# Three layer-norm joints of a two-block transformer kernel: GpSimd makes the shift, two engines empty PSUM in turn, modulation rows and kept rows are placed elsewhere

## The reference

```python
def first_block(x, ...):
    for l in range(2):
        mix = token_mixing(x, w_in[l], ...)              # attention branches, then @ w_o
        x = layer_norm(ALPHA * x + mix, ln1_g[l], ln1_b[l])
        ffn = conv_ffn(x, w_up[l], conv_w[l], conv_b[l], w_down[l])
        x = layer_norm(ALPHA * x + ffn, ln2_g[l], ln2_b[l])
    return x

def second_block(x, c, ctx, c_ctx, ada_w, ada_b, ...):
    for i in range(2):
        m_lat = silu(c) @ ada_w[i] + ada_b[i]            # modulations, width 6 * 1024
        m_ctx = silu(c_ctx) @ ada_w[i] + ada_b[i]
        h = _rms(x, norm1_g[i]) * (1.0 + sc1) + sh1      # slices of m_lat, m_ctx
        ...
```

## Time and profile before

| | |
|---|---|
| median of 3 runs | 3923.62 us (3922.15 to 3926.23) |
| the profiled execution's own time | 3922.99 us |
| its span, from first to last instruction | 3920.8 us |
| PE busy, share of the span | 3644.1 us, 93% |
| DVE busy | 2035.2 us, 52% |
| ACT busy | 1444.3 us, 37% |
| POOL busy | 185.0 us, 5% |

### The profile page before, as it was taken

One profiled execution on the slowest core, in us unless ns is written; L12 is line 12 of the kernel. 1 busy time (PEld: TensorE's weight loads), 2 busy tenths in 40 slices (PEclk: granted clock), 3 DMA queues, 4 the chain that ended last, 5 costly groups with the idle time before them and its releaser, 6 DMA issues.

```text
span 3920.8 us, 49215 instructions
## 1 busy us (share of the span) xinstructions
PE 3644.1 (93%) x19410; PEld 2923.5 (75%) x19410; DVE 2035.2 (52%) x3634; ACT 1444.3 (37%) x2248; POOL 185.0 (5%) x267
## 2 busy tenths in 40 slices
PE   8889998899979999998999887999999979899999
PEld 6676676687756766776878765788888879777887
DVE  4645656767865456577772445342222352564333
ACT  3445642443133446424431325331112233553222
POOL 0000000100010000001000110100000122000000
PEclk9989998999989899998999898899999999999999
DMA  4111233323521112343333100011211111212222
GB/s 167 61 68 51 86 116 131 124 107 149 194 104 66 70 54 76 111 155 123 129 126 116 72 22 1 33 54 49 81 49 70 66 55 55 71 49 75 106 93 81
DMA packets 65943, 339.95 MB, mean 87 GB/s; under 512 B 6832, under 2 KB 8368, under 8 KB 39984
## 3 DMA queue, kind: packets, MB, share of 16 engines
q1 hardware_dynamic: 65712, 336.82, 23.6%
HBM read 328.40 MB, written 8.39 MB: 86 GB/s over the span
## 4 chain that ended last, share of the span: by engine, by line
PE 73%; DVE 15%; ACT 8%; issue 2%; POOL 1%; DMA 1%; DVEq 0%; ACTq 0%; SPq 0%; POOLq 0%
PE ps L1710 22%; PE ps L1711 21%; PE ps L1712 21%; DVE wl L1956 3%; PE ps L1699 2%; PE ps L1832 2%; DVE junk L2001 2%; PE ps L1719 2%; ACT wh L1851 2%; PE ps L1825 1%; DVE tt L1964 1%; DVE u L1956 1%; DVE hl L1964 1%; ACT opb L1944 1%; PE ps L1726 1%
## 5 line engine op out<-in xcount | busy, mean ns | idle before, releaser
L1956 DVE TENSOR_TENSOR wl<-raw,wh 128x2048 fp32r<-128x2048 f32 (+2 forms) x275 | 549.7, 1999 | 431.8 <-ACT wh L1851 412.1
L1851 ACT ACTIVATE wh<-raw 128x2048 fp32r<-128x2048 f32 (+2 forms) x275 | 457.2, 1663 | 792.0 <-PE ps L1712 788.3
L1710 PE MATMUL ps<-hh,wh 128*128 128x512 f32 (+1 forms) x1248 | 446.3, 358 | 11.0 <-DVE hl L1964 9.4
L1711 PE MATMUL ps<-hl,wh 128*128 128x512 f32 (+1 forms) x1248 | 443.6, 355 | 0.0
L1712 PE MATMUL ps<-hh,wl 128*128 128x512 f32 (+1 forms) x1248 | 443.2, 355 | 0.0
L1710 PE MATMUL ps<-xhb,wh 128*128 128x512 f32 x832 | 370.5, 445 | 11.7 <-DVE xlb L1956 10.9
L1711 PE MATMUL ps<-xlb,wh 128*128 128x512 f32 x832 | 338.2, 407 | 0.0
L1712 PE MATMUL ps<-xhb,wl 128*128 128x512 f32 x832 | 336.8, 405 | 0.0
L1710 PE MATMUL ps<-xha,wh 128*128 128x512 f32 x704 | 283.8, 403 | 23.8 <-DVE wl L1956 21.2
L1711 PE MATMUL ps<-xla,wh 128*128 128x512 f32 x704 | 282.5, 401 | 0.0
L1712 PE MATMUL ps<-xha,wl 128*128 128x512 f32 x704 | 281.9, 400 | 0.0
(11 more groups left out here) (282 smaller groups left out, 6956.1 us busy)
## 6 DMA issues: line engine op xcount, KB each, us to landing
raw<-in_wts SPq DMA_DIRECT2D x199, 1024.0 KB, 4.8
lt<-in_wts SPq DMA_DIRECT2D x110, 512.0 KB, 3.4
raw<-in_wts SPq DMA_DIRECT2D x44, 512.0 KB, 3.4
raw<-in_wts SPq DMA_DIRECT2D x28, 448.0 KB, 3.1
x_scratch<-xt SPq DMA_DIRECT2D x3, 2048.0 KB, 9.1
xt<-x_scratch SPq DMA_DIRECT2D x3, 2048.0 KB, 8.0
oe<-in_relb SPq DMA_DIRECT2D x16, 384.0 KB, 3.5
bt<-in_big SPq DMA_DIRECT2D x1, 2688.0 KB, 9.3
```

The source lines that it names most:

```text
L1710: T.matmul(u.out, u.sh, u.mh, start=u.first, stop=False)
L1711: T.matmul(u.out, u.sh, u.ml, start=False, stop=False)
L1851: A.activation(u.h, u.raw, ACT.Copy).then_inc(*act.inc())
L1956: V.tensor_tensor(o_, a, b, op).then_inc(*dve.inc())
```

## The change

Seven things are different.

1. `ln_scale`: DVE negates the mean in a small instruction of its own. POOL multiplies it by the inverse deviation, and ACT waits for POOL. DVE no longer waits for POOL.
2. The odd chunks of `ln_split` are now read from PSUM by DVE (`ln_shift`, a `tensor_scalar` into a third pair of buffers `tz`), and ACT makes the high part from that copy in SBUF (`ln_halves`). Even chunks stay as they were.
3. The `wl` of the next panel is forced out of the queue `lows` ahead of the turning of tiles.
4. Modulation panels: none directly ahead of a layer norm or in the first panels behind one. In layer 1 they stand after each `up` panel from the sixth on, where before two of three had one; and 10 stand in the `down` stage of layer 1, which had none.
5. `gain`: multiply and add are both done on DVE, one tile per panel (steps 20, 36, 52, 68 instead of 6, 11, 16, 21).
6. The rings of PSUM banks start again at bank 0 after a joint.
7. In the mixing, the first users of one scratch region wait until the kept rows are stored.

```diff
-            add_ada()
+            if l == 0 or part == "dv":
+                add_ada()
...
-                add_ada(2)
+                add_ada((2, 2, 1, 0)[2 * half + kk])
...
-            if j % 3 == 0 or l and j % 3 == 1:
+            if j >= 5 and (l or j % 2):
                 add_ada()
...
-                if l == 0:
+                if half == 0 and (l == 0 or q < 5) or l == 0 and q < 3:
                     add_ada(2)
...
+            held[:] = [Rec(a=2048, n=2048, free=stored[0])] if stored[0] else []
...
+            run_later(lows, force=True)
...
+            def shift(k):
+
+                j = 1 + k // 2 % 2
+                u = add("ln_shift", t=TZ[j], t_free=tt_free[j], **parts(k))
+                banks[k].free = [DVE(u)]
+
+            def halves(k):
+                if k % 2:
+                    j = 1 + k // 2 % 2
+                    u = add("ln_halves", t=TZ[j], h=XH[:, k, :], l=XL[:, k, :], came=banks[k].free[0])
+                else:
+                    j = 0
+                    u = add("ln_split", t=TZ[0], t_free=tt_free[0], h=XH[:, k, :], l=XL[:, k, :], **parts(k))
+                    banks[k].free = [ACT_(u)]
+                x_ks[k] = DVE(u)
+                tt_free[j] = [DVE(u)]
...
+                shift(1)
+                for k in range(0, 8, 2):
+                    if k < 6:
+                        shift(k + 3)
+                    halves(k)
+                    halves(k + 1)
+            FR.n = GR.n = 0
...
-                    later(small, 6 + 5 * i, gain)
+                    later(small, 20 + 16 * i, gain)
...
-                    act.wait_ge(*at(DVE(u)))
+                    act.wait_ge(*at(POOL(u)))
...
-                    dve.wait_ge(*at(POOL(u)))
-                    stt(u.rs[:, 14:15], u.rs[:, 12:13], -1.0, u.rs[:, 15:16], ALU.mult, ALU.mult)
+                    ts(u.rs[:, 12:13], u.rs[:, 12:13], -1.0, None, ALU.mult)
+                elif kind == "ln_shift":
+                    dve.wait_ge(*at(u.came))
+                    dve.wait_ge(*prm)
+                    for t in u.t_free:
+                        dve.wait_ge(*at(t))
+                    ts(u.t, u.b, u.scale, u.bias, ALU.mult, ALU.add)
...
+                    dve.wait_ge(*u.b_t)
+                    tt(u.x, u.x, u.b, ALU.add)
...
+                    pool.wait_ge(*at(DVE(u)))
+                    tt(u.rs[:, 14:15], u.rs[:, 12:13], u.rs[:, 15:16], ALU.mult)
...
-                    pool.wait_ge(*at(DVE(u)))
-                    tt(u.x, u.x, u.b, ALU.add)
```

More of the change, by code:

```diff
@@ L1086, in layer_norm @@
             run_later(turns, force=True)
-            TZ = [buf(f"tz{l}{which}{j}", [P, S], M0 + 30720 + 512 * j)[:, :] for j in range(2)]
+            TZ = [buf(f"tz{l}{which}{j}", [P, S], M0 + 30720 + 512 * j)[:, :] for j in range(3)]
             z_t = [None] * 4
@@ L1117, in layer_norm, with parts @@
                                              came=z_t[i], less=int(k0 == 0), free=banks[k].free + [tab] if i == 0 else [], end=i == 3))
-            tt_free = [[], []]
-            for k in range(8):
+            def parts(k):
                 b = banks[k]
-                wb = dict(b=b.ap, bias=gb[:, 8 + k:9 + k], scale=gb[:, k:k + 1], came=turned_t[k])
-                if last2:
-                    u = add("ln_last", x=XX[:, k, :], **wb)
-                    x_ks[k] = ACT_(u)
-                else:
-                    u = add("ln_split", t=TZ[k % 2], t_free=tt_free[k % 2], h=XH[:, k, :], l=XL[:, k, :], **wb)
-                    x_ks[k] = DVE(u)
-                    tt_free[k % 2] = [DVE(u)]
-                b.free = [ACT_(u)]
-                if last2:
-                    early["sums"](k, x_ks[k])
+                return dict(b=b.ap, bias=gb[:, 8 + k:9 + k], scale=gb[:, k:k + 1], came=turned_t[k])
+            tt_free = [[], [], []]
+            def shift(k):
[12 more added lines that the diff above has]
+                tt_free[j] = [DVE(u)]
+            if last2:
+                for k in range(8):
+                    u = add("ln_last", x=XX[:, k, :], **parts(k))
+                    x_ks[k] = ACT_(u)
+                    banks[k].free = [ACT_(u)]
+                    early["sums"](k, x_ks[k])
+            else:
+                shift(1)
[5 more added lines that the diff above has]
+            FR.n = GR.n = 0
             x_ready = x_ks[7]
@@ L1139, in gain @@
                             pg.done(DVE(u))
-                            pb_.done(POOL(u))
-                            add("load", dst=xkeep.rearrange("(i p) n -> p i n", p=P), src=XT[:, :, :], sem=s_xd, free=[POOL(u)])
+                            pb_.done(DVE(u))
+                            add("load", dst=xkeep.rearrange("(i p) n -> p i n", p=P), src=XT[:, :, :], sem=s_xd, free=[DVE(u)])
                             nxd[0] += 1
                             stored[0] = (s_xd, 16 * nxd[0])
-                    later(small, 6 + 5 * i, gain)
+                    later(small, 20 + 16 * i, gain)
         def ffn1(l):
@@ L1913, in act_program @@
                     A.activation(u.h, u.b, ACT.Identity, bias=u.bias, scale=u.scale).then_inc(*act.inc())
+                elif kind == "ln_halves":
+                    act.wait_ge(*at(u.came))
+                    act.wait_ge(*act.own())
+                    A.activation(u.h, u.t, ACT.Copy).then_inc(*act.inc())
                 elif kind == "up_conv":
```

4 lines of the change are left out of this document (1 added, 3 removed).

## The result

The changed kernel takes 3867.71 us (median of 4 runs, 3866.16 to 3871.71) against 3922.89 us before (4 runs, 3921.35 to 3926.23): a ratio of 0.986 with a 95% interval of 0.9843 to 0.9877. The profiled execution took 3866.16 us, its span 3864.3 us, 56.5 us less than that of before; the prediction had 3865.8. So PE's pauses were shortened, while its work stayed: PE is busy for 16 us less (work at the lower clock that went) and has as many instructions.

What follows compares the result with a forecast made beforehand. PE, busy for 93% of the span, was taken as the bound; 64.0 us won at the joints less 9.0 lost in layer 1's `up` stage gave 55.0, hence 3869 us, with 8 in 10 for 3858 to 3885.

Steps and rivals of the forecast that it cites:

- Joints 1 and 3: PE's pauses at these two joints: each keeps 14.3 us, so 21.2 and 22.1 us are won.
- the POOL detour no longer matters: Tile statistics at the joints: POOL's second operation costs at most 0.66 us, so ACT reaches the last tile after it.
- a sign of being wrong: In the profile after: ACT waiting for POOL at a tile would mean the shift on POOL is on the path.
- Forcing `wl` out early is what removes the 7.51 us wait: Second panel behind joint 1: `wl` runs 2.2 to 4.5 us after PE's last dense matmul, while DVE is idle.
- Joint 2: PE's pause at this joint: 38.4 us falls to 19.7, so 18.7 us are won.
- The term for rope: In joint 2: two pairs of rope matmuls (3.9 us) and waits of 0.8 and 0.3 us for ACT's copy stay.
- Joint 4: Tiles gain 0.1 us and `wl` moves ahead of the turnings, where PE waited 1.79 us: 2.0 us won.
- The `up` stage: Layer 1: modulation rows in 16 successive panels put DVE 0.65 us behind in each; 9.0 us lost.
- Rival A: Layer 1's `up` stage holds its pace as DVE finds 0.65 us a panel: no 9.0 us loss, 3860; chance 0.12.
- Bank rings ... cost nothing; at most 1 us: The bank rings, with the moves within `wo` and the mixing and the stored-rows wait, cost at most 1 us.
- Two engines in turn: Chunks at the joints, ACT and DVE alternating: some 2.5 us a pair, hidden behind the turnings; next to nothing gained.
- kept rows on DVE: Adds leave POOL: each of 12 blocks costs DVE at most 1.22 us more, which lies in its slack.

Runs made afterwards that it cites:

- The plan alone: The kernel before with only the new places of the modulation rows: 3904.98 us, ratio 0.9953.
- the last kernel: The changed kernel with rings not restarted, rows spread, none in the last two `wo` panels, `wh` moved among the chunks, `wl` behind them: 3840.15 us, ratio 0.978.

## Why the prediction was right, and where it was not

**The whole.** 3869 against 3867.71, in the range. It is right by its mechanism in most of its parts, and by errors that cancel in the rest: joints 2 and 4 gave 8.8 us more, `wo` and the second half of `down` took 6.3, joints 1 and 3 and the `up` stage 2.1, and the mixing and the second block together gave 2.3.

**Joints 1 and 3** (21.2 and 22.1; measured 20.6 and 21.3). What joint 4 showed of before did carry over: ACT's 1.75 us a tile, one tile behind the other after the `wh`. Within it one term was too small: the last turning came at T0 + 10.1, not 8.2. The step that failed is "the POOL detour no longer matters", with "the second POOL operation costs at most the 0.66 us": POOL's multiply was priced from a row where nothing ran beside it, while the change puts a 2.29 us instruction with two SBUF inputs beside it. The prediction had the rule on the lock in hand and used it for the kept rows alone. And it had DVE's time wrong: the last tile "could start at about T0 + 3.3", and the forced `wl` "runs at about T0 + 2.2 to 4.5". That is DVE's time in joint 2. In joints 1 and 3 one modulation panel is left ahead of the last residuals, and the `wl` starts at T0 + 6.9, just when ACT comes to the last tile. At the predicted time the lock would have cost nothing, if joint 2 is a guide. ACT waits for POOL there by 2.00 us, which the prediction had named as a sign of being wrong. What comes behind the first dense matmul hid part of it: I had put 1.9 us there (0.4 and 1.5), and it is 15.1 - 14.3 = 0.8.

**"Forcing `wl` out early is what removes the 7.51 us wait"** failed. The plan alone took that wait to 0.93 us, and the changed kernel without the forcing doesn't wait at all. Eight modulation rows (6.6 us of DVE) ahead of the residuals and eight behind the chunks made it; with them gone, `wl` is done 1.1 us before PE needs it. The credit belongs to the plan.

**Joint 2** (18.7; measured 24.3). The term for rope was mis-sized: the waits of 0.8 and 0.3 us that were to stay are one of 0.41, and the pairs of rope matmuls, taken over at 2.08 us, ran at the higher clock. The 1.5 us for slow matmuls behind the pause came to 0.1 (the first dense matmul is followed by the next after 0.33 us, at 1072.63). And 0.6 us was won behind the stretch that was summed up, where a wait of 0.96 us at 1150.75 went. PE, joint 2 after:

```profile
1068.12 4.44 PE L1816 MATMUL ps<-ct,xt 128*128 128x128 f32 x20 [0.64 <-ACT xt L1925]
...
1083.75 1.13 PE L1752 MATMUL ps<-gs,ct 128*128 128x512 f32 x2
...
1094.18 1.13 PE L1752 MATMUL ps<-gs,ct 128*128 128x512 f32 x2 [0.41 <-ACT gs L1891]
```

The pair costs 1.13 us at a granted clock of 1.00, not 2.08 at 0.50: the pauses of 5.89 and 8.03 us ahead of the pairs are gone. Here the last turning is at T0 + 8.2 as predicted (T0 = 1059.89). POOL's multiply takes 1.89 us in this joint too, but it starts at T0 + 2.7 (1062.55) instead of T0 + 7.4, since DVE was free earlier, and ends before ACT comes to that tile.

**Joint 4** (2.0; measured 5.2). The wait of 1.79 us went, as predicted (2.4 us with what hangs on it); another 2.8 us came from turnings and first sums at the higher clock, which I had not counted and which three of the other kernels (the plan alone, all chunks through ACT, adds on POOL) don't show. That part is luck.

**The `up` stage** (9.0; measured 9.7). Right in place, pace and size. Waits begin one panel later than said, ahead of the fourteenth (13 panels of 11.17 us behind the first dense matmul at 1739.8), and come every 11.84 us. The stall behind them sits at the first `down` panel (4.33 us) instead of the second (5 to 6), since the restarted ring gives PE a bank that DVE still reads. Rival A, that DVE finds the 0.65 us, is rejected; spreading the rows removed all of it. The rows in the `down` stage were not quite "free": in its second half PE waits 0.85 us for a `wl` (2067.53) that DVE makes behind two modulation panels and four residuals, and loses 1.1 us in every kernel with the new plan.

**"Bank rings ... cost nothing; at most 1 us"** failed: 5.2 us in the `wo` stage of layer 1. There PE needs a bank that DVE has only just left. I had looked at banks in the joint where the restart stands, and not at the stages behind it, whose banks it shifts too.

**Two engines in turn, kept rows on DVE**: 2.6 us in all, and 0.3 us a joint at most. For the adds that is nothing; for the two engines "next to nothing by itself" was a little low, 1.5 us in joint 2.

**Left open.** What places the low-clock stretches in the second block, 9 us between the best and the worst of these executions, wasn't tried; as one kernel's runs differ by up to 10.3 us, it need not be the kernel. Not tried either: the kept rows moved back alone, and the changed kernel with no modulation rows ahead of the last residuals of joints 1 and 3. Nor were two versions of the last kernel: one whose DVE starts the third residual earlier, and one with the ring restart in joint 3 alone.

## What to carry to other kernels

Price a small instruction by what will run beside it after the change, not by its row in the old trace: a multiply of one column was 0.19 us alone and 1.89 us next to a two-input instruction of VectorE. In joints 1 and 3 that was on PE's path; in joint 2 the same 1.89 us cost nothing, as they fell 4.7 us earlier. So work out when the two meet, too. For an in-order engine compute the round (its work per panel) against the panel, and count how many rounds the lead lasts; a share of 82% busy was already too much. When a joint has one engine that begins with a wait for the end of the stage, look for what stands behind that wait without needing it: moving it in among the chunks, together with fewer rows ahead of the residuals, won another 12.5 us.

## What the hardware showed that I had not expected

- GpSimd's 128 x 1 multiply: 0.19 us, and 1.89 us beside a 2.29 us `wl`, in joints 1 to 3 alike; 0.19 us again when that `wl` was held back or not forced.
- A `tensor_scalar` of 128 x 512 from PSUM (`ln_shift`) took 0.81 us, where I had taken 0.69 from `scalar_tensor_tensor` with one operand in PSUM; on ACT the same reading is 0.78.
- The second block, 1674 us with the same matmuls in the same order, differed by up to 9.3 us between the profiled executions of these kernels (-5.2 to +4.1 against before), nearly all of it in how long PE's matmuls took (1565.1 to 1575.0 us busy).
- Behind the wait of 4.33 us the next matmuls stand 0.42 to 0.43 us apart (1998.53, 1998.95) instead of 0.23, so this wait costs more than its length. Behind the waits of 0.38 us in the `up` stage the granted clock stays at 1.00.
